# Two pairs' q and k by block products, a conv norm by streamed squares, and attention's steps in another order

## The reference

```python
h = rms_norm(x, g_pre_mix)
hc, bg, cg, q, k, v = split(h @ w_in, 6)              # each 1024 x 512
u = cg * hc
y_conv = bg * (u * w[2] + shift(u, 1) * w[1] + shift(u, 2) * w[0])
y_attn = band_attention(q, k, v, rel_bias)            # 8 heads of 64, chunks of 64, 8 chunks to the left
y = concat(group_norm(y_conv, g_conv, 8), group_norm(y_attn, g_attn, 8)) @ w_out
x = x + rms_norm(y, g_post_mix)
gate, up = split(rms_norm(x, g_pre_ffn) @ w_ffn_in, 2)
return x + rms_norm((silu(gate) * up) @ w_ffn_out, g_post_ffn)
```

## Time and profile before

| what | value |
|---|---|
| median of 3 runs | 1108.61 us (1108.59 to 1108.73) |
| the profiled execution | 1108.71 us |
| its span in the trace | 1106.7 us |
| TensorE busy | 1096.9 us, 99% |
| VectorE, ScalarE, POOL busy | 759.8, 467.3, 162.4 us |
| granted TensorE clock, mean | 0.999 of full speed |

### The profile page before, as it was taken

The page is one execution under the profiler, slowest core; times in us unless marked ns, Lnnn a source line. Parts: engine busy times, 40 slices in busy tenths (PEclk is TensorE's granted clock), DMA queues, the critical chain, the costliest instruction groups (busy, mean ns, idle before and its releaser), DMA issues.

```text
span 1106.7 us, 15974 instructions
## 1 busy us (share of the span) xinstructions
PE 1096.9 (99%) x5653; PEld 909.5 (82%) x5653; DVE 759.8 (69%) x1206; ACT 467.3 (42%) x818; POOL 162.4 (15%) x258
## 2 busy tenths in 40 slices
PE   9999999999999999999999999999999999999997
PEld 7888888878888888888888888888888888888886
DVE  6878854354546656868787777878787786555584
ACT  6542333555555655734322232323223256444441
POOL 3300022010101220312112211211221110000031
PEclk9999999999999999999999999999999999999999
DMA  7332216300100444535546445543644689776632
GB/s 272 107 120 75 58 57 224 119 20 20 39 3 19 163 162 133 172 95 174 159 142 209 136 122 187 177 146 114 218 136 152 214 307 377 232 237 223 218 114 79
DMA packets 116182, 164.10 MB, mean 148 GB/s; under 512 B 7752, under 2 KB 73304, under 8 KB 116128
## 3 DMA queue, kind: packets, MB, share of 16 engines
q1 hardware_dynamic: 98496, 103.30, 29.3%
q0 software_dynamic: 16464, 55.89, 14.4%
q10 hardware_dynamic: 1168, 4.20, 1.0%
HBM read 119.56 MB, written 46.94 MB: 150 GB/s over the span
## 4 chain that ended last, share of the span: by engine, by line
PE 98%; ACT 1%; DVE 1%; DMA 0%; issue 0%; DVEq 0%; POOL 0%; POOLq 0%
PE psum L1278 34%; PE psum L1305 18%; PE psum L872 12%; PE psum L1111 10%; PE psum L1162 8%; PE psum L1023 4%; PE psum L915 3%; PE psum L896 2%; PE psum L886 2%; PE psum L861 1%; PE psum L999 1%; PE psum L923 0%; PE psum L1005 0%; PE psum L905 0%; ACT arena L1514 0%; PE psum L992 0%
## 5 line engine op out<-in xcount | busy, mean ns | idle before, releaser
L1278 PE MATMUL psum<-arena_r,ws 128*128 128x512 f32 x960 | 224.1, 389 | 0.0
L1278 PEld LDWEIGHTS psum<-arena_r,ws 128*128 128x128 f32 x960 | 180.3, 188 | 37.3
L1278 PE MATMUL psum<-hT,ws 128*128 128x512 f32 x720 | 169.9, 389 | 0.0
L1278 PEld LDWEIGHTS psum<-hT,ws 128*128 128x128 f32 x720 | 135.2, 188 | 27.9
L872 PE MATMUL psum<-hT,ws 128*128 128x512 f32 (+1 forms) x624 | 142.2, 380 | 0.6 <-ACT arena L1540 0.6
L1305 PE MATMUL psum<-hT 128*128 128x512 f32 (+1 forms) x600 | 135.2, 385 | 0.0
L1305 PEld LDWEIGHTS psum<-hT 128*128 128x128 f32 x600 | 111.3, 188 | 22.5
L872 PEld LDWEIGHTS psum<-hT,ws 128*128 128x128 f32 x624 | 107.9, 189 | 19.9 <-issue 0.8
L2408 DVE TENSOR_TENSOR misc<-misc,psum 128x512 f32<-128x512 f32 x100 | 68.6, 686 | 48.3 <-PE psum L1278 46.0
L1729 ACT ACTIVATE ws<-o_raw 128x512 fp32r<-128x512 f32 x40 | 25.1, 627 | 139.1 <-DVE o_raw L2386 138.6
L1162 PE MATMUL psum<-ws,hT 128*128 128x512 f32 x348 | 81.8, 393 | 0.0
(11 more groups left out here) (263 smaller groups left out, 1557.7 us busy)
## 6 DMA issues: line engine op xcount, KB each, us to landing
raw<-in_w_ffn_in SPq DMA_DIRECT2D x44, 512.0 KB, 4.2
act_scratch<-arena POOLq DMA_DIRECT2D x77, 256.0 KB, 3.2
raw<-in_w_in SPq DMA_DIRECT2D x22, 512.0 KB, 3.8
arena<-in_w_ffn_out POOLq DMA_DIRECT2D x22, 512.0 KB, 5.6
arena<-act_scratch SPq DMA_DIRECT2D x38, 256.0 KB, 3.3
arena<-in_x SPq DMA_DIRECT2D x16, 512.0 KB, 6.3
raw<-in_w_out SPq DMA_DIRECT2D x16, 512.0 KB, 3.4
raw<-act_scratch SPq DMA_DIRECT2D x26, 256.0 KB, 3.2
```

What stands on the lines that cost most here:

```text
L1278: last = mm(blocks(bank), w[:, k * P:(k + 1) * P], b_operand(i, part, k), start=fresh_bank and k == 0 and w is hi and part == 0, stop=k == ...
```

## The change

- **Front.** `FRONT_PAIRS = 2`: q and k of pair 1 get a round of their own (round 5; pair 0's is now round 6). Its results are put together in rows 18 and 17 (by `stage_c11` on ScalarE and the sums on VectorE), stored to DRAM and read back into rows 13 and 14. The chunks that the pieces work on fall from 8 to 6 (`FILLED`).
- **Conv norm.** The squares are split into a high part (`high_sq`, ScalarE) and a low one (`low_sq`, VectorE). A constant 128 x 128 matrix with 1/64 in each head's block is held still, and the squares stream through, two halves by two parts: the mean square stands in PSUM for each element. ScalarE takes `Abs_reciprocal_sqrt` of it, VectorE refines the root by a Newton step and multiplies the row (`mix_row`). GpSimd, the spread and the transposes have no part in it any more. The fourth row keeps its old way.
- **Attention.** Each step on TensorE is now scores, output, pieces, transposes; step 0 begins with its pieces; the output of tiles 6 and 7 moves behind the next pair's first scores, its turning back to step 1. `AHEAD` is 4 and `FILLS` is new. ScalarE's and VectorE's steps follow: halves are drained in the step in which they end, `read_pT` stands between the two exponentials, the sum of squares moves from step 2 to 3, `o_scale` from 3 to 4, the three taps of the fourth row follow the draining of its half at once. Conv rows are read back behind the second load of `w_out`.

```diff
-    OUT0 = 2 * PAIRS
+    FRONT_PAIRS = 2
+    FILLED = 2 * (PAIRS - FRONT_PAIRS) + 2
+    OUT0 = FILLED
...
-    FRONT = 6
+    FRONT = 5 + FRONT_PAIRS
...
-        AHEAD = 3
-        FILLS = [[1] + [2] * 7 + [1]] * LAST + [[1] + [2] * 4 + [1] * 4]
+        AHEAD = 4
+        FILLS = [[1, 1, 1, 1, 2, 1, 1, 1, 2], [1, 1, 1, 1, 1, 1, 1, 2, 2], [1, 1, 1, 1, 2, 1, 1, 1, 1], [1, 1, 2, 1, 1, 2, 1, 1, 2]]
```

TensorE:

```diff
             def step(t, s):
                 if s == 0:
+                    fill(t, s)
                     pe.wait_ge(qk_ready, t * 2 + 2)
-                if s == 3 and t == 0:
-                    pe.wait_ge(v_back, 64)
-                if s in (3, 5, 7):
-                    output(t, s - 3)
                 if scored(t, s):
...
                 if s == 0 and t > 0:
-                    turn_back(t - 1, NT - 2)
+                    output(t - 1, NT - 2)
+                if s == 3 and t == 0:
+                    pe.wait_ge(v_back, 64)
+                if s in (3, 5, 7):
+                    output(t, s - 3)
...
+                if s == 0:
+                    return
+                if s < NT or t < LAST:
+                    fill(t, s)
+                pe.wait_ge(exp_done, unit(t, 2 * s))
+                if s > 1:
+                    pe.wait_ge(pT_act, tile(t, s - 1))
...
+                if s == 1 and t > 0:
+                    turn_back(t - 1, NT - 2)
+                transpose_p(t, s - 1)
+                if s == 1 and t > 1:
+                    pe.wait_ge(tile_free, tile(t - 1, NT - 2) + 2)
+                    transpose_o(t - 1, OT_BANKS)
+                if s == NT and t == LAST:
+                    fill(t, s)
                     output(t, NT - 2)
...
             def stats(t):
 
-                pe.wait_ge(conv_sq, t + 1)
...
+                pe.wait_ge(conv_mixed, means_split(t))
                 if t > 0:
-                    pe.wait_ge(conv_mixed, t)
-                conv_norms(PP[2], 0, NT).then_inc(conv_norm, 1)
-
-            behind = {(4, 1): (stats, 0), (4, 3): (stats, 1), (4, 4): (norms, 0),
-                      (5, 0): (norms, 1), (5, 1): (stats, 2), (5, 4): (norms, 2)}
+                    pe.wait_ge(conv_mixed, mixed(t - 1))
+                for half in range(2):
+                    for part in (CR, CU):
+                        last = mm(PP[2][:, half * HALF:(half + 1) * HALF], same_head, row_r(part)[:, half * HALF:(half + 1) * HALF],
+                                  start=(part == CR), stop=(part == CU))
+                last.then_inc(conv_stat, 1)
+
+            behind = {(4, 2): 0, (5, 0): 1, (5, 5): 2}
```

ScalarE:

```diff
-                act.wait_ge(*((front_out, n) if n else (t_lo, NT)))
+                act.wait_ge(*((t_lo, NT) if n == 0 else (front_out, n) if n < 6 else (c12_made, n)))
                 go(u2, BANK[0], ACT.Copy).then_inc(p1_copied, 1)
...
+                go(row_r(CR), row(CU), ACT.Copy).then_inc(conv_sq, 1)
+
+            def conv_roots(t, bank):
+
+                act.wait_ge(conv_stat, t + 1)
+                go(row(CR), bank, ACT.Abs_reciprocal_sqrt, bias=eps_col[:, 0:1]).then_inc(conv_root, 1)
...
+            square_y(0), front_copy_first(4), high_sq(0)
+            front_high(5, 0), conv_roots(0, PP[2]), square_y(1), high_sq(1)
+            for i in range(1, 7):
+                front_high(5, i)
+            conv_roots(1, PP[2]), front_copy_first(5), square_y(2)
+            front_high(6, 0), stage_c11(5), high_sq(2)
+            front_high(6, 1), front_high(6, 2), conv_roots(2, PP[2])
```

VectorE:

```diff
+            def low_sq(t):
+                dve.wait_ge(conv_sq, squared(t, 1))
+                tt(row_r(CU), row(CU), row_r(CR).bitcast(F32), ALU.subtract).then_inc(conv_mixed, 1)
+
+            def mix_row(t):
+
+                f, mean, y = row(CR), PP[2], row(CONV_ROWS[t])
+                dve.wait_ge(conv_root, t + 1)
+                chain(stt(mean, mean, EPS, f, ALU.add, ALU.mult))
+                chain(stt(mean, mean, -0.5, f, ALU.mult, ALU.mult))
+                chain(stt(f, mean, 1.5, f, ALU.add, ALU.mult))
+                stt(y, y, params[:, t, 3:4], f, ALU.mult, ALU.mult).then_inc(conv_mixed, 1)
...
+            low_sq(0)
             make_u2(4)
             front_low(5, 0)
-            conv_stats_read(0)
             make_u3(4)
-            front_s(5)
...
+            mix_row(0)
             dve.wait_ge(prod, multiplied(4, 3))
             times(2, 0, BANK[0]).then_inc(c11_done, 1)
...
             make_c22(4, tiles_of(row(CV), 1), 1)
-            conv_stats_read(1)
-            front_low(5, 4)
+            front_s(5)
+            front_low(5, 1), front_low(5, 2), front_low(5, 3)
             make_c21(4, tiles_of(row(CV), 0), 0)
-            conv_mix(0)
-            front_low(5, 6)
+            low_sq(1)
+            front_low(5, 4), front_low(5, 5)
             make_c12(4)
             times(2, 1, u2).then_inc(front_out, 1)
...
+            for n in range(5, FRONT - 1):
+                q_row, k_row = [row(r) for r in QK_STAGED]
+                make_u2(n)
+                if n == 5:
+                    mix_row(1)
+                make_u3(n)
+                front_low(n + 1, 0)
+                if n == 5:
+                    dve.wait_ge(conv_stored[1], 16)
+                else:
+                    dve.wait_ge(qk_stored, 32 * (n - 5))
+                make_c22(n, tiles_of(k_row, 1), 1)
+                if n == 5:
+                    low_sq(2)
+                front_s(n + 1)
+                front_low(n + 1, 1), front_low(n + 1, 2), front_low(n + 1, 3)
+                make_c21(n, tiles_of(k_row, 0), 0)
+                if n == 5:
+                    mix_row(2)
+                front_low(n + 1, 4), front_low(n + 1, 5)
...
+            def drain(t, s):
+
+                for h in halves_done(t, s):
+                    if h // 2 >= CG:
+                        read_half(h // 2, h % 2)
+                        if h == 2 * CG + 1:
+                            tap(LAST, 0), tap(LAST, 1), tap(LAST, 2)
```

ScalarE's step:

```diff
+                if s > 0:
+                    drain(t, s)
+                    read_pT(t, s - 1)
+                if s < NT:
                     exp(t, 2 * s + 1)
...
-                if s == 1 and t > 0:
-                    high_in(2 * t + 1)
+                if s == 2 and t > 0:
                     square_pair(t - 1)
-                if not more and s == 3:
+                if not more and s == 5:
                     act.wait_ge(o_var, t)
                     squares(t, (0, 1))
```

SyncE:

```diff
+            for n in range(1, 7):
+                next_front(n)
             store_conv(0), store_conv(1)
...
+            for slot in range(2):
+                sp.wait_ge(front_lo, split(FRONT - 1, (3, 5)[slot]))
+                load_filled(slot)
+            store_qk(FRONT - 2)
+            if FRONT == 7:
+                store_conv(2)
```

More of the change, by code:

```diff
@@ L595, in _, with next_front @@
             store_v(3, 2, v_stored[1]), store_v(5, 2, v_stored[1]), store_v(7, 1, v_stored[1])
-            for n in range(1, FRONT):
+            def next_front(n):
                 for slot in range(2):
@@ L621, in _ @@
                 load(g % 2, wout_d[m * P:(m + 1) * P, :])
+                if g == OUT0 + 1:
+                    sp.wait_ge(qk_ready, 2 * PAIRS)
+                    for t in range(PAIRS - 1):
+                        load_conv(t)
                 if g == OUT0 + 4:
@@ L742, in o_norm_factors @@
                 factors_to(rst[:, :], o_eps[:, :], UNITS, o_rs, t + 1)
-            for t in range(PAIRS - 1):
-                conv_norm_factors(t)
             pool.wait_ge(prod, multiplied(FRONT - 1, 4))
@@ L946, in output, with fill @@
                 times_v(t, i)
+            def fill(t, s):
+                for q in range(pieces_ahead(t, s), pieces_ahead(t, s + 1)):
+                    piece(q)
             def step(t, s):
                 if s == 0:
+                    fill(t, s)
                     pe.wait_ge(qk_ready, t * 2 + 2)
-                if s == 3 and t == 0:
-                    pe.wait_ge(v_back, 64)
-                if s in (3, 5, 7):
-                    output(t, s - 3)
                 if scored(t, s):
@@ L1137, in _ @@
                     if (n, i) in behind:
[L1138 to L1139 removed]
+                        stats(behind[n, i])
             for q in range(AHEAD):
@@ L2162, in read_half @@
                     dve.wait_ge(half_used, g + 1)
-                out = row(CV if j else CU, HALF, at)
+                out = row(CU if g == CG else CV, HALF, at)
                 tt(out, half_bank(), row(CV, HALF, at), ALU.mult).then_inc(half_free[half], 1)
@@ L2201, in step @@
                     add_bias(t, 2 * s + 1)
+                if 0 < s < NT:
+                    drain(t, s)
+                if s == 0 and t > 0:
+                    copy_o(t - 1, NT - 2)
+                if s in (3, 5, 7):
+                    copy_o(t, s - 3)
+                if s == NT and not more:
+                    o_finish(t, PP[1])
                 if s > 4:
                     read_pT(t, s - 1)
```

(38 more changed lines are left out.)

282 lines of the change are left out of this document (142 added, 140 removed).

## The result

The changed kernel takes 1124.40 us (median of 4 runs, 1122.89 to 1124.52) against 1108.62 for the kernel before (4 runs, 1108.59 to 1108.73): a ratio of 1.0139, with 95% from 1.0121 to 1.0157. It is slower, as forecast, but by 15.8 us and not by 2.8, and the time lies outside the range of 1103.0 to 1115.0. The profiled execution took 1124.3 with a span of 1122.5.

A forecast was written before the change was run, and what follows sets the result against it. TensorE, busy 99% of the span, was taken as the bound. Work -8.48, front waits +3.5 and attention waits +8.4 gave +3.4, less 0.6 for overlap +2.8: 1111.4 us, range 1103.0 to 1115.0.

The forecast's parts named there:

- TensorE's own work: Conv norm saves 5.76 and moving q, k of pair 1 saves 2.72 net: -8.48 us together.
- Front waits: New TensorE waits in front rounds 5 and 6, 1.0 and 2.5: +3.5 us together.
- The table load: ScalarE's load for the new roots: hidden if late; if ahead of the first roots, up to 1.3, or 2.7 with a drain.
- Start: Start of attention: the next piece waits for the half's drain, +1.0, and the second scores for the biases, +1.1.
- step 3: Output of tiles 0 and 1 waits for ScalarE's read with nothing between, 0.7 in each of 4 pairs: +2.8.
- taps: Pair 3, step 2: taps right after the drain delay biases and copy_o, so TensorE's turn back waits: +2.0.
- pair ends: Between the transposes of tiles 6 and 7 ScalarE's work is uncovered: +0.6 in pair 2, +0.9 in pair 3.
- old waits: Attention's earlier waits taken back by the new order: 1.3 that the profile names and some 0.8 unlisted, -2.1.
- Covered: Only the start's waits and half the front's stay, the rest of attention as full as before: 1103.9 us; chance 0.28.
- Break-even: Two thirds of both the front's and attention's wait sums: 1108.0 us, from 1106 to 1109.5; chance 0.24.
- VectorE bounds rounds 5 and 6: Front: a slower mix_row form (1.6 instead of 1.31) or a store 2 us later adds more wait: 1115 us; chance 0.12.
- The likeliest case: The forecast itself: the walked waits outweigh the work saved, 1111.4 us, its own range 1109.5 to 1113.5; chance 0.33.

The follow-up runs named there:

- x8: The changed kernel with the attention's steps in the order of the kernel before, filling laid evenly in 2 or 3 row blocks per step; 1107.16 us.
- x9: x8 with VectorE in front round 5 taking the last sum and the split behind it ahead of mixing row 2; 1105.09 us.
- x3: The changed kernel with VectorE taking the low part of each streamed weight chunk one attention step later; 1119.48 us.
- x1: The changed kernel with extra TensorE matmuls or transposes ahead of its three waits of about 2 us, results spoiled; 1121.03 us.
- x5: The changed kernel with the edits of x2, x3 and x4 together; 1113.00 us.
- x2: The changed kernel with pair 3's three taps moved back to the ends of steps 3 and 4; 1119.68 us.
- x6: x5 plus tile 0's scores ahead of piece 4 at the start, and half a piece each side of step 3's output; 1109.88 us.
- x7: The kernel before, own order, one of two row blocks left out in every second piece (21.8 us less TensorE work, projections incomplete); 1091.81 us.
- x4: The changed kernel with VectorE in step 8 draining the C gate's finished half before the low part of the next k; 1119.94 us.
- x12: x8 with whole pieces again, one or two to a step; 1107.17 us.

## Why the prediction was wrong

**TensorE's own work, right.** TensorE is busy for 160.24 us in the attention of x8; before it was 182.07, and 182.07 - 21.76 = 160.3. The front grew by 16.1 against 16.8.

**Front waits, right in place, too large.** 3.5 forecast, 2.4 measured: 1.7 at the fourth product of round 6 (2.5 forecast) and 0.7 for the row squares ahead of the means (1.0 forecast, at the first product of round 5). The chain behind the first is shown by x9. The front came out only 0.7 below the forecast, so 0.4 of its growth has no place in the walk, and that the sum fitted so well is in part luck. The mixing form is no slower with its output in PSUM: 1.23 in the row of x9 above, 1.28 taken.

**The table load.** The profile has two, of which none is waited for:

```profile
143.82 1.28 ACT L1549 ACT_TABLE_LOAD   x1
...
206.09 1.28 ACT L1616 ACT_TABLE_LOAD   x1
```

The first stands ahead of the roots while ScalarE waits for the means, the second while it waits for the first bias. So the cost is nothing, the value taken. The 1.3 for an early load did not come about, and neither did the 2.7 that followed from the Trainium skill (ScalarE: Activation LUTs, "What ACT_TABLE_LOAD costs"); the drain of which that page speaks shows in neither row. Behind the first load there is no room for the page's 1.38: the load ends at 145.10 and the roots start at 146.25, 1.15 later, as soon as the means are done. No run here had a load that TensorE waited for.

**Attention's walked waits, right at each place that the walk named alone.** Start 2.1 forecast, 0.78 and 1.02 measured; step 3 four times 0.7, measured 0.73, 1.43, 0.69 and 0.69, where the 1.43 has 0.7 of the low part's delay in it; taps 2.0 and 1.92; pair ends 0.6 and 0.9, measured 0.53 and 1.05. Without the 2.1 for old waits the walk came to 10.5; the same places measured 15.5 - 2.1 - 0.9 - 0.7 - 1.9 = 9.9.

**The step that failed** is the judgement on the steps that the walk passed over. The prediction says "In the steady steps 4 to 7 the new order is good: the filler between scores and transposes gives the exponential a whole step", and that "no chain is longer"; and under *Ends of pairs* it walks only ScalarE's read and exponential. It looked at the scores, the exponential and the copies alone, and not at the operations that come once in a chunk or a pair and share their queues. Two were missed:
- The low part of a weight chunk, which stands ahead of the next step's biases in VectorE's queue and waits for ScalarE's high part: 2.1 + 0.9 + 0.7 = 3.7 of waits.
- The drain of the C gate's first half behind low_k in step 8: 1.9.

The first is not new as such. Before the change both halves were taken in one step too, and VectorE waited even longer for the high part, 2.79, at no cost to TensorE. From the timeline of the kernel before, a chunk in pair 2:

```profile
296.25 1.03 ACT L1523 ACTIVATE arena<-psum 128x1024 f32<-128x1024 f32 x1 [2.87 <-PE psum L896]
...
298.80 1.04 ACT L1347 ACTIVATE ws<-raw 128x1024 fp32r<-128x1024 f32 x1
...
299.87 1.23 DVE L1854 TENSOR_TENSOR ws<-raw,ws 128x1024 fp32r<-128x1024 f32 x1 [2.79 <-ACT ws L1347]
300.57 1.14 PE L886 MATMUL psum<-ws 64*128 64x384 f32 x12
...
301.76 0.82 DVE L2134 CUSTOM_DVE_ANT_0 arena<-psum,arena 128x640 f32<-128x640 f32 x1 [0.34 <-issue]
```

The low part is over at 301.1, before the scores are (301.7), so the bias loses nothing. ScalarE's copy, which follows the transposes, starts 4.3 ahead of the next scores, since the pieces and the output stand between. In the new order the transposes stand last in the step: the copy starts at 311.19, 0.1 behind the start of the next scores (311.08), the low part ends at 315.2, and the bias starts at 315.15, 2.9 after the scores are over. That this order is what makes the wait is read from these rows; x3 shows only that the low part's place sets it. With the old order restored (x8) the same chunk in the same step makes VectorE wait 2.57; TensorE's scores wait for nothing there, but the output behind them waits 1.30.

**The clock had no term.** The earlier trace rows show it at 1.00, and the forecast took TensorE's time to be work plus waits. Here the three longest waits, 1.92 to 2.14, were each followed by a stretch at 1.2 GHz that cost 1.7 more: 5.1 us. x1 shows the cause by adding work. And the 0.6 for overlap went the wrong way: TensorE's busy time in attention, less the clock's 5.1, is 162.4 against the 160.3 of the work itself. These 2.1 us go with the new order, for x5 has 162.2 at full clock and x8 160.2 with the same matmuls; that many short breaks cost them is likely, but not shown.

3.7 + 1.9 + 5.1 + 2.1 = 12.8, and attention was 13.0 us longer than forecast (-0.4 against -13.4). Two small errors nearly cancel in the rest: the walked waits came out 0.6 shorter, and the 0.8 of old waits "that no list names" was not there to take back. Of its signs, the one for "wrong", attention under 163 us, pointed the other way: it looked for a forecast too high, and none stood for one too low.

**The rivals.** *Covered* and *Break-even* assumed that a wait here is saved there. x2 to x6 show the reverse: what was taken away was won nearly whole, so the waits were in series. *VectorE bounds rounds 5 and 6* did not happen (1.23 for its form). The likeliest case held the mechanism, order in one queue, and left out two of its places and what a long wait brings behind it.

**What stays open.** How much the norm alone is worth was not tried: in the last front round the split of one operand stands in the row where the squares are, so that without a seventh round the third row's norm has no place. Together with x7 one can bound the pieces: moving q, k of pair 1 saves 21.8, costs 19.0 and opens waits of 4 to 5 us even in the old order. x8 keeps a wait of 1.30 that the low part still causes, and x6 two behind `o_scale`; neither was mended. What decides whether a wait of 1.9 is followed by the low clock was not settled.

## What to carry to other kernels

When steps are reordered, walk each in-order queue with all that is in it, the operations that come once in a chunk or a pair above all, and ask of each whether it waits for another engine while something urgent stands behind it; an operation that waits harmlessly in one order (VectorE's 2.79 before) can cost its wait in another, so its end has to be set against the next moment at which something behind it is wanted; a split whose halves are on two engines is safer at a distance from its other half. When filling work is taken away, a TensorE wait as long as these is to be costed with a stretch at half clock behind it; where nothing else can cover it, even useless work there is cheaper than idling. And an experiment that thins the old kernel (x7) tells in one run whether the amount of work can be the loss.

## What the hardware showed unexpectedly

- After the changed kernel's three TensorE waits of 1.92 to 2.14 us its granted clock fell to 1.2 GHz for some 3.4 us each, beginning 0.6 to 1.1 us after the engine was busy again; work of 6 matmuls took 2.83 there instead of 1.66:

```profile
352.59 2.83 PE L935 MATMUL psum<-hT,ws 128*128 128x512 f32 x6
```

- The same wait (1.92) in x2 brought no such stretch, and neither did the wait of 1.7 in round 6, in any of the ten profiles that have it. One stretch more or less fits the scatter of 1.6 to 2 us between runs of the changed kernel, x3 and x4, whose mean clocks differ with it (0.994 and 0.996 in the changed kernel), while x5 and x12, without long waits in attention, scatter by 0.5 to 0.7.
- Extra transposes and matmuls, about 1.4 us ahead of each of the three waits, made the kernel 3.4 us faster (x1).
